# Expert sums held in four PSUM banks, one pool for the pre-activations, and a freed row buffer, in a one-core attention, retention and mixture-of-experts block

## The chip, the cores and the metric

The kernel runs on one core of one Trainium2 chip. The metric is the device time of one execution in microseconds. All numbers below come from three timed runs of the kernel before and from one profiled execution of it.

## The reference, cut to what matters

One transformer layer over 256 tokens of width 1024, in float32. The front part (attention over selected keys beside retention, one output projection, residual) is followed by a mixture of experts, and that is where nearly all the time goes:

```python
h2 = rms_norm(x, norm2_gain)
logits = h2 @ w_router + b_router             # 32 experts
top_val, top_idx = lax.top_k(logits, 4)       # each token goes to 4 of them
combine = one_hot(top_idx) weighted by softmax(top_val)
for e in range(32):
    z = h2 @ w1[e] + b1[e]                    # 1024 x 2048
    glu = minimum(z[..., 0::2], 7); lin = clip(z[..., 1::2], -7, 7)
    act = glu * sigmoid(1.702 * glu) * (lin + 1)
    out += combine[:, e] * (act @ w2[e] + b2[e])   # 1024 x 1024
x = rms_norm(x + out, final_gain)
```

The weights of an expert are 8 MB (w1) and 4 MB (w2), and all 32 experts are read once in a sweep: 402.7 MB.

## The kernel before, in words

**Stages.** The projections, the attention and the retention come first. TensorE then projects the output (L1272), the residual goes into `acc`, ScalarE copies it in another column order into `h2` (`copy_half`, L558), the router picks four experts for each token, and `place` (L875) gives each token a rank among the tokens of its expert. A sweep over the 32 experts follows; each has 64 slots, and a second sweep is run only if an expert has more tokens than that.

**One expert.** In `step` (L1469), for expert e, TensorE does, in an order written out by hand: the bias rows of z (`z_bias`, L1304), eight rows of w1 (`z_rows`, L1359; a "row" is 1 MB of weights, four matmuls), and between these rows the work of its neighbours: the gather of the tokens of expert e+1 (`gather`, L1344) and its transpose, the transpose of the activation of expert e-1 (`act_T`), the transposes of the gates, and after every second expert the scatter of the pair before (`scatter`, L1424). The step ends with `down` (L1384), the sixteen matmuls of w2 for expert e-1. VectorE reads z out of PSUM (`swiglu`, L961) and ScalarE applies the sigmoid and copies results out of PSUM.

**PSUM, before.** The z of even experts is in banks 0 and 1, that of odd ones in banks 2 and 3. The outputs of `down` and of the scatters share banks 4 and 5. After each scatter VectorE adds its 128x512 results to `acc` (`add_back`, L976), and TensorE waits for that. Only the last four experts are summed in PSUM, in banks 0 to 3: `final` opens these sums with zero matmuls (`open_sum`, L1442) and VectorE puts `acc` into them (`base_sum`, L1006).

**The weights' queue.** SyncE issues all weight loads in one order, each behind a wait for the buffer that it overwrites (`w1_used` counts rows of w1 that TensorE is done with, `w2_used` quarters of w2). w1 has 16 rows of buffer (two experts), w2 has four. By the time the experts begin, expert 0 and 1 are there, with w2 of expert 0 and one row of expert 2, which lies where a row of expert 0 would be; that row of expert 0 has a place in `arena`. From then on the queue goes by what TensorE frees: rows 0 to 6 of expert 2 as `w1_used` reaches 1 to 7, expert 3 at 9, 10, 12, 14 and 16, w2 of expert 1, the two halves of expert 4 at 20 and 24, w2, the halves of expert 5 at 28 and 32, and so on.

**The end.** `last_w2` (L325) puts w2 of experts 30 and 31 into rows of w1. `final` (L1517) runs the last expert and the last three `down`s. Then both token tiles are normalised and stored in four quarters, all issued by SyncE.

Of the kernel before, what the change touches and what calls it, by code (L numbers as in the profile page):

```python
# [21 lines left out]
P = 128  # L22
# [30 lines left out]
def constants():  # L53
# [12 lines left out]
    before = (np.arange(P)[:, None] < np.arange(P)[None, :]).astype(np.float32)  # L66
# [6 lines left out]
            "c_rank": np.concatenate([before, ones], 1), "c_onehot": onehot}  # L73


def hybrid_block(nc, x, norm1_gain, w_in, rel_bias, idx_k_ln_gain, idx_k_ln_bias, ret_gn_gain, w_out,
# [3 lines left out]
    with ctx:  # L80
# [10 lines left out]
        h2 = sb("h2", [P, TT, D])  # L91
# [29 lines left out]
        h2flat = h2[:, :, :].rearrange("p a b -> p (a b)")  # L121
        hT = carve(h2flat, 0, [KD, S])
# [42 lines left out]
        before, ones = carve(arena, 3400, [P]), carve(arena, 3528, [P])  # L165
# [49 lines left out]
        h2_ready = sem("h2_ready"); x2_tr = sem("x2_tr"); x2T_act = sem("x2T_act"); x2T_dve = sem("x2T_dve"); wr_ready = sem("wr_ready"); route_mm = sem("route_mm")  # L215
        top_ready = sem("top_ready"); ex_done = sem("ex_done"); chosen_ready = sem("chosen_ready")
        rank_mm = sem("rank_mm"); count_mm = sem("count_mm"); sweeps_ready = sem("sweeps_ready")
# [12 lines left out]
        gT_tr = sem("gT_tr"); gT_sb = sem("gT_sb"); scattered = sem("scattered"); added = [sem(f"added{t}") for t in range(TT)]  # L230
        shifted = sem("shifted")
        y_dve = sem("y_dve"); part_sum = sem("part_sum"); based = sem("based"); fin_sq = sem("fin_sq"); fin_inv = sem("fin_inv"); fin_root = sem("fin_root"); res_ready = sem("res_ready")
        last_dma = sem("last_dma")

# [13 lines left out]
        def _(sp):  # L248
# [26 lines left out]
            sp.dma_start(w1r[:, 6, :], w1_v[0, 1, 1, :, 0:2048]).then_inc(w1_in[3], 16)  # L275
            sp.dma_start(w1r[:, 7, :], w1_v[2, 1, 1, :, 2048:4096]).then_inc(w1_in[3], 16)
# [19 lines left out]
            sp.dma_start(before, c_rank[:, 0:P]).then_inc(rank_in, 16)  # L296
# [41 lines left out]
            def rest_of_sweep(base):  # L338
# [23 lines left out]
                by_row(3, 1, range(2))  # L362
                next_w1(base, 3, 1, range(1, 4))
# [34 lines left out]
            sp.wait_ge(fin_root, 3)  # L398
            sp.dma_start(out_v[:, 1, 512:1024], res[:, 1, 512:1024]).then_inc(last_dma, 16)
# [50 lines left out]
        def _(act):  # L450
# [105 lines left out]
            def copy_half(t, c):  # L556

                nc.scalar.activation(h2[:, t, :].rearrange("p (j c q) -> p c j q", j=4, c=2)[:, c],  # L558
                                     acc[:, t, 512 * c:512 * c + 512].rearrange("p (q j) -> p j q", j=4), ACT.Copy).then_inc(h2_ready, 1)

# [4 lines left out]
            copy_half(0, 0)  # L565
            copy_half(0, 1)
# [4 lines left out]
            copy_half(1, 0)  # L571
            copy_half(1, 1)
# [7 lines left out]
            for i in range(2):  # L580
                nc.scalar.activation(hg[:, 256 * i:256 * i + 256], ps[:, 4, 256 * i:256 * i + 256], ACT.Copy).then_inc(first_copied, 1)
# [3 lines left out]
            def take_hg(base, e):  # L585

                act.wait_ge(gathered, base + e)
                nc.scalar.activation(hg, ps[:, 6, :], ACT.Copy).then_inc(hg_sb, 1)  # L588
# [11 lines left out]
            def take_y(base, e, par):  # L600
                act.wait_ge(w2_used, 4 * base + 4 * (e + 1))
                lo = 64 * par
                nc.scalar.activation(ysb[lo:lo + 64, 0, :], ps[lo:lo + 64, 4, :], ACT.Copy)  # L603
                hi = 64 - lo
                nc.scalar.activation(ysb[hi:hi + 64, 1, :], ps[hi:hi + 64, 5, :], ACT.Copy).then_inc(y_sb, 1)

            def take_y_half(base, e, par, bank=4):
# [5 lines left out]
            def take_gateT():  # L613
                act.wait_ge(first_made, 3)
                nc.scalar.activation(gateT[:, :], ps[:, 4, 0:P], ACT.Copy).then_inc(first_copied, 1)

            def take_gT(half_base, m, to=gT):
                act.wait_ge(gT_tr, half_base + m + 1)
                nc.scalar.activation(to, ps[:, 6, :].rearrange("p (a n) -> p a n", a=2), ACT.Copy).then_inc(gT_sb, 1)

            def step(base, hb, m, par, first=False, last=False):
# [4 lines left out]
                if not (first and par == 0):  # L626
                    take_act(base, e - 1)
                if par == 1:
# [4 lines left out]
            def final(base, hb):  # L633
# [5 lines left out]
                take_y_half(base, NE - 3, 1)  # L639
                take_act(base, NE - 1, actT_last)  # L640
                nc.scalar.activation(spare[:, 0:1], spare[:, 1:2], ACT.Sqrt)
                take_y_half(base, NE - 2, 0)
                take_y_half(base, NE - 1, 1, bank=6)

            def sweep(base, hb, start=False):
# [3 lines left out]
                if start:  # L649
                    take_gateT()  # L650
# [18 lines left out]
            act.wait_ge(part_sum, 4 * n)  # L669
# [3 lines left out]
            act.wait_ge(scattered, n * NE)  # L673
# [5 lines left out]
            nc.scalar.activation(res[:, 1, 512:1024], res[:, 1, 512:1024], ACT.Copy, scale=st[:, 7:8]).then_inc(fin_root, 1)  # L679

        @block.vector
        def _(dve):
# [228 lines left out]
            def count_sweeps():  # L911

                dve.wait_ge(count_mm, 1)
                link(v.tensor_reduce(st[0:1, 76:77], ps[0:1, 5, 0:NE], AX.X, ALU.max))
# [46 lines left out]
            def swiglu(base, e, zb, free=True, lin=lin):  # L961
# [14 lines left out]
            def add_back(hb, j, t):  # L976

                for c in range(2):
# [630 lines left out]
```

## Time and profile before

| | |
|---|---|
| time of three runs | 1081.39, 1081.69, 1081.77 us; median 1081.69 |
| the profiled execution's own time | 1080.58 us |
| its span, first to last instruction | 1078.8 us (1.78 us lie around it) |
| TensorE matmul busy | 1037.1 us, 96% of the span |
| VectorE, ScalarE, GpSimd busy | 302.9, 157.0, 22.2 us |
| moved by DMA | 429.79 MB, mean 398 GB/s |
| mean granted TensorE clock | 0.988 |

Busy time of TensorE is not TensorE at its peak, and the page shows matmul busy and DMA busy both near full for most of the span: the table alone doesn't say which of the two sets the time of a stage. Waits and the pace of the loop do.

### The profile page before, as it was taken

The numbers are of one execution on the slowest core, as the hardware profiler recorded it, in microseconds if no ns is written. First come the engines' busy times: TensorE is split into PE (matmuls) and PEld (weight loads), VectorE is DVE, ScalarE is ACT, GpSimd is POOL, SyncE is SP. The second block draws the span as 40 slices with busy tenths as digits, with TensorE's granted clock in tenths as the row PEclk, the third lists the DMA queues.
The fourth block names the chain that finished last, engine by engine and source line by source line (L and its number), as shares of the span: only waits on it lengthen the run. The fifth ranks groups of instructions, "written<-read, shape, count | busy, mean of one in ns | idle before, by whom it ended". The sixth has DMA issues, their size and how long they took to land.

```text
span 1078.8 us, 11542 instructions
## 1 busy us (share of the span) xinstructions
PE 1037.1 (96%) x4616; PEld 400.2 (37%) x4616; DVE 302.9 (28%) x704; ACT 157.0 (15%) x282; POOL 22.2 (2%) x29
## 2 busy tenths in 40 slices
PE   8999999999999999999999999898989899999997
PEld 7458454333333333333333333332333333333332
DVE  2555622422222222222221312221223222221231
ACT  1231333110111111101010111011101101011111
POOL 1212000000000000000000000000000000000000
PEclk9999999999999999999998999999999999999999
DMA  9886948999999999999999999999999999999995
GB/s 327 244 254 263 385 166 317 396 435 425 427 426 433 435 428 433 430 428 429 434 433 430 432 427 433 433 435 430 429 431 434 434 430 429 435 434 431 423 426 235
DMA packets 33066, 429.79 MB, mean 398 GB/s; under 512 B 4908, under 2 KB 6352, under 8 KB 16368
## 3 DMA queue, kind: packets, MB, share of 16 engines
q1 hardware_dynamic: 31120, 426.03, 93.7%
q10 hardware_dynamic: 1216, 1.70, 1.1%
q0 software_dynamic: 704, 1.71, 0.6%
q8 instruction: 17, 0.28, 0.1%
q14 instruction: 9, 0.07, 0.0%
HBM read 426.80 MB, written 2.62 MB: 398 GB/s over the span
## 4 chain that ended last, share of the span: by engine, by line
PE 67%; DMA 30%; DVE 1%; issue 1%; SPq 0%; ACT 0%; ACTq 0%; DVEq 0%
PE ps L1370 28%; DMA w1r<-w_mlp 23%; PE ps L1398 13%; DMA w2r<-w_mlp 6%; PE ps L1439 5%; PE ps L1348 3%; PE ps L1099 3%; PE ps L1111 3%; DMA w1r<-w_out 1%; PE ps L1166 1%; PE ps L1412 1%; PE ps L1272 1%; PE ps L1131 1%; PE ps L1241 1%; PE ps L1356 1%; PE ps L1378 1%
## 5 line engine op out<-in xcount | busy, mean ns | idle before, releaser
L1370 PE MATMUL ps<-w1r,arena 128*64 128x512 f32 x2040 | 483.5, 610 | 22.4 <-DMA w1r<-w_mlp 22.1
L1370 PEld LDWEIGHTS ps<-w1r,arena 128*64 128x64 f32 x2040 | 141.9, 139 | 283.7 <-issue 277.3
L1398 PE MATMUL ps<-w2r,arena 128*64 128x512 f32 x960 | 212.1, 593 | 7.6 <-DMA w2r<-w_mlp 7.6
L1398 PEld LDWEIGHTS ps<-w2r,arena 128*64 128x64 f32 x960 | 68.2, 137 | 147.3 <-issue 131.4
L982 DVE TENSOR_TENSOR acc<-ps,acc 128x512 f32<-128x512 f32 x56 | 36.1, 686 | 173.5 <-PE ps L1439 173.5
L974 DVE TENSOR_TENSOR arena<-arena 128x512 f32<-128x512 f32 x32 | 22.2, 692 | 163.5 <-ACT arena L594 163.4
L598 ACT ACTIVATE arena<-ps 128x512 f32<-128x512 f32 x31 | 18.5, 597 | 288.7 <-PE ps L1378 288.6
L936 DVE TENSOR_TENSOR arena<-ps,cols 128x512 f32<-128x512 f32 x31 | 21.4, 692 | 139.1 <-PE ps L1356 139.1
L1348 PE MATMUL ps<-h,arena 128*64 128x512 f32 x248 | 58.7, 592 | 0.0
L603 ACT ACTIVATE arena<-ps 64x512 f32<-64x512 f32 x29 | 17.2, 592 | 269.6 <-PE ps L1398 269.6
L1439 PE MATMUL ps<-arena 128*128 128x512 f32 x112 | 55.5, 618 | 0.0
L957 DVE TENSOR_SCALAR arena<-small,rank,gate 128x64 f32<-128x64 f32 x128 | 31.3, 309 | 58.1 <-PE ps L1466 58.1
L588 ACT ACTIVATE arena<-ps 128x512 f32<-128x512 f32 x31 | 18.5, 597 | 158.4 <-PE ps L1348 158.4
L968 DVE TENSOR_SCALAR arena<-ps 128x512 f32<-128x512 f32 x32 | 33.5, 1048 | 13.2 <-PE ps L1370 13.2
L927 DVE TENSOR_SCALAR sel_z<-small 96x64 bf16 (+1 forms) x30 | 5.7, 190 | 103.1 <-PE ps L1370 103.1
L969 DVE TENSOR_SCALAR arena<-ps 128x512 f32<-128x512 f32 x32 | 33.9, 1061 | 0.0
L1439 PEld LDWEIGHTS ps<-arena 128*128 128x128 f32 x112 | 19.0, 189 | 36.0 <-issue 36.0
L1348 PEld LDWEIGHTS ps<-h,arena 128*64 128x64 f32 x248 | 18.8, 137 | 34.9 <-issue 34.3
L1111 PE MATMUL ps<-h,w1r 128*128 128x256 f32 x128 | 28.1, 380 | 0.0
L1099 PE MATMUL ps<-w1r,h 128*128 128x512 f32 x64 | 27.8, 592 | 0.0
L1111 PEld LDWEIGHTS ps<-h,w1r 128*128 128x128 f32 x128 | 24.2, 190 | 3.3
L1378 PEld LDWEIGHTS ps<-small,arena 128*128 128x128 f32 x128 | 13.4, 140 | 26.0 <-issue 26.0
(259 smaller groups left out, 604.1 us busy)
## 6 DMA issues: line engine op xcount, KB each, us to landing
w1r<-w_mlp SPq DMA_DIRECT2D x54, 4096.0 KB, 30.9
w2r<-w_mlp SPq DMA_DIRECT2D x32, 2048.0 KB, 18.1
w2r<-w_mlp SPq DMA_DIRECT2D x14, 4096.0 KB, 20.5
w1r<-w_mlp SPq DMA_DIRECT2D x17, 2048.0 KB, 9.6
w1r<-w_in SPq DMA_DIRECT2D x6, 2048.0 KB, 19.0
w1r<-w_mlp SPq DMA_DIRECT2D x12, 1024.0 KB, 7.8
w1r<-w_out SPq DMA_DIRECT2D x2, 2048.0 KB, 13.8
w1r<-w_in SPq DMA_DIRECT2D x2, 1024.0 KB, 10.6
```

Source lines behind the costliest of these rows:

```text
L957: ins = v.tensor_scalar(gated[:, t, which, at:at + 64], slotn, rank[:, t, bass.ds(e, 1)], gate[:, t, bass.ds(e, 1)], ALU.is_equal, ALU.mult)
L968: v.tensor_scalar(g3, z[:, :, :, 0], 7.0, None, ALU.min).then_inc(glu_ready, 1)
L969: v.tensor_scalar(l3, z[:, :, :, 1], 7.0, -7.0, ALU.min, ALU.max).then_inc(z_read, 1)
L974: v.tensor_tensor(lin, lin, sig, ALU.mult).then_inc(act_ready, 1)
L982: ins = v.tensor_tensor(sl, ps[:, 4 + c, :], sl, ALU.add)
L1099: ins = mm(ps[:, bank + t, 0:n], hT[:, k, P * t:P * t + P], w[:, k, 0:n], start=(k == 0), stop=(k == KD - 1))
L1111: ins = mm(ps[:, bank + g // 2, S * (g % 2):S * (g % 2) + S], w[:, k, P * g:P * g + P], hT[:, k, :], start=(k == 0), stop=(k == KD - 1))
L1348: ins = mm(ps[64 * c:64 * c + 64, 6, :], onehotP[:, par, t, :], h2[:, t, :].rearrange("p (j c q) -> p c j q", j=4, c=2)[:, c], start=(t == ...
L1370: ins = mm(ps[64 * c:64 * c + 64, 2 * par + n, :], hgT[:, par, k % 4, 64 * (k // 4):64 * (k // 4) + 64], cols_z, start=False, stop=(k == 7))
L1378: ins = nc.tensor.transpose(ps[:, 7, P * j:P * j + P], lin[:, P * j:P * j + P], ident)
L1398: ins = mm(ps[at:at + 64, 4 + c, :], actT[:, k % 4, 64 * (k // 4):64 * (k // 4) + 64], w2r[:, k // 2, col:col + 512], start=(k == 0), stop ...
L1439: ins = mm(ps[:, 4 + c, :], gT[:, c, P * t:P * t + P], ysb[:, c, :], start=not with_bias, stop=True)
```

## The change

1. **z in one pair of banks.** z of every expert is in banks 4 and 5 (expert 1 alone in 2 and 3, `z_bank`). `z_bias` of an expert now waits until VectorE has read z of the expert before. `down` writes both halves into bank 6; gather, transposes and gate transposes share bank 7.
2. **Sums in banks 0 to 3 from the first scatter on.** `open_sum` and `base_sum` run once, inside expert 2's step. Every scatter adds to these banks; `add_back` and the waits on it are gone.
3. **`h2` is gone.** Gathers read `acc` directly, and ScalarE puts the columns in order when it copies the gathered tokens out of PSUM (`take_hg`, and the two first copies, now with a stride of four elements). The freed buffer, `hx`, holds a row of expert 0; expert 2's last pair of rows is loaded as a whole beforehand. At `w1_used` 7 `hx` takes row 7 of expert 3, and row 6 of expert 3 is issued at `w1_used` 15 in place of a pair at 16.
4. **Around the start.** Ranks count the tokens behind instead of ahead, which gives the count per expert with one small VectorE operation in `place` and spares two matmuls. The z bias of expert 1 moves ahead of the first expert, `gate_T` into expert 1's step behind row 6. `keep_busy` matmuls stand at a few places of the front part.
5. **The end.** A new order in `final`; the pair 28 is added at the end of expert 30's step; the last quarter of the output is issued by ScalarE.

```diff
+        def z_bank(base, e):
+            return 2 if isinstance(base, int) and isinstance(e, int) and e == 1 else 4
...
             sp.wait_ge(proj_done, 5)
-            sp.dma_start(w1r[:, 6, :], w1_v[0, 1, 1, :, 0:2048]).then_inc(w1_in[3], 16)
-            sp.dma_start(w1r[:, 7, :], w1_v[2, 1, 1, :, 2048:4096]).then_inc(w1_in[3], 16)
+            load_w1(2, 3, 3)
...
             sp.wait_ge(proj_done, 8)
             load_w1(0, 2, 2)
+            sp.dma_start(hx[:, :], w1_v[0, 1, 1, :, 0:2048]).then_inc(w1_in[3], 16)
...
                     sp.wait_ge(w1_used, 7)
-                    sp.dma_start(w1r[:, 6, :], w1_v[2, 1, 1, :, 0:2048]).then_inc(w1_in[3], 16)
+                    sp.dma_start(hx[:, :], w1_v[3, 1, 1, :, 2048:4096]).then_inc(w1_early, 16)
+                    by_row(3, 1, range(2))
+                    next_w1(base, 3, 1, range(1, 3))
+                    sp.wait_ge(w1_used, 15)
+                    sp.dma_start(w1r[:, 14, :], w1_v[3, 1, 1, :, 0:2048]).then_inc(w1_in[7], 16)
...
-            sp.wait_ge(fin_root, 3)
-            sp.dma_start(out_v[:, 1, 512:1024], res[:, 1, 512:1024]).then_inc(last_dma, 16)
...
-            copy_half(0, 0)
-            copy_half(0, 1)
...
             for i in range(2):
-                nc.scalar.activation(hg[:, 256 * i:256 * i + 256], ps[:, 4, 256 * i:256 * i + 256], ACT.Copy).then_inc(first_copied, 1)
+                nc.scalar.activation(hg[:, 256 * i:256 * i + 256].rearrange("p (j q) -> p j q", j=2),
+                                     ps[:, 0, :].rearrange("p (q j) -> p j q", j=4)[:, 2 * i:2 * i + 2], ACT.Copy).then_inc(first_copied, 1)
...
+            act.wait_ge(fin_root, 3)
+            act.dma_start(out[0].rearrange("(t p) d -> p t d", p=P)[:, 1, 512:1024], res[:, 1, 512:1024]).then_inc(last_dma, 16)
...
                 dve.wait_ge(mm_done, count)
+                if t == TT - 1:
+                    v.tensor_tensor(lw[0:1, 0, 0:NE], ps[0:1, 6, 64 + NE:64 + 2 * NE], chosen[0:1, t, :], ALU.add)
...
-            def add_back(hb, j, t):
...
+            def base_sum(t):
+
+                dve.wait_ge(opened, t + 1)
+                v.tensor_copy(ps[:, 2 * t:2 * t + 2, :].rearrange("p b n -> p (b n)"), acc[:, t, :]).then_inc(based, 1)
...
+            def keep_busy(n, bank):
+
+                for i in range(n):
+                    mm(ps[:, bank, :], bias3[:, 0:P], bias3[:, 0:512], start=True, stop=True)
...
             gather_first(1).then_inc(first_made, 1)
-            mm(ps[:, 5, 0:NE], ones, chosen[:, 0, :], start=True, stop=False)
-            mm(ps[:, 5, 0:NE], ones, chosen[:, 1, :], start=False, stop=True).then_inc(count_mm, 1)
+            z_bias(0, 1, 1, free=False)
...
+            keep_busy(1, 0)
...
                 if free:
-                    pe.wait_ge(z_read, base + e - 1)
+                    pe.wait_ge(z_read, base + e)
...
                 for c in range(2):
-                    ins = mm(ps[:, 4 + c, :], gT[:, c, P * t:P * t + P], ysb[:, c, :], start=not with_bias, stop=True)
-                ins.then_inc(scattered, 1)
+                    ins = mm(ps[:, 2 * t + c, :], gT[:, c, P * t:P * t + P], ysb[:, c, :], start=False, stop=False)
...
+                if isinstance(base, int) and isinstance(m, int) and (m, par) == (1, 0):
+                    pe.wait_ge(first_copied, 3)
+                    for t in range(TT):
+                        open_sum(t)
...
+                if par == 1 and first and isinstance(base, int):
+                    gate_T()
                 if par == 1:
                     gates_T(base, hb, m)
...
+                if last:
+                    pe.wait_ge(y_sb, base + e - 1)
+                    pe.wait_ge(gT_sb, hb + m)
+                    for t in range(TT):
+                        add_expert(t, 0, gT)
```

`final` on TensorE after the change, from its start (`add_expert` is two matmuls over 64 rows, `down_late` the `down` from rows of w1):

```python
z_bias(base, e, 1)
for k in range(5): z_rows(base, e, lap, k, 1, False)
act_T(base, e - 1)
for k in range(5, 7): z_rows(base, e, lap, k, 1, False)
gates_T(base, hb, NE // 2 - 1)
z_rows(base, e, lap, 7, 1, False)
down(base, wb, e - 2, 1)
act_T(base, e, lin_last)
down_late(0, 0, actT_30, range(4), {0: 0}, hb, 4)
for t in range(TT): add_expert(t, 1, gT)
down_late(0, 0, actT_30, range(4, 8), {4: 1}, hb, 4)
down_late(1, 4, actT_last, range(4), {0: 2}, hb, 5)
add_expert(0, 0, gT_last)
down_late(1, 4, actT_last, range(4, 8), {4: 3, 6: 4, 7: 5}, hb, 5)
add_expert(1, 0, gT_last)
add_expert(0, 1, gT_last, stop=True)
add_expert(1, 1, gT_last, stop=True)
```

## Rows read from the trace of the kernel before

**Rows 1.** The page, GB/s of the DMA engines in 40 slices of 27 us
```profile
GB/s 327 244 254 263 385 166 317 396 435 425 427 426 433 435 428 433 430 428 429 434 433 430 432 427 433 433 435 430 429 431 434 434 430 429 435 434 431 423 426 235
```

**Rows 2.** The chain that ended last: start, us, what; first rows of a step
```profile
347.16 3.44 PE ps L1370 x16
...
400.49 3.44 PE ps L1370 x16
...
685.25 3.65 PE ps L1370 x16
...
743.53 5.35 PE ps L1370 x16
```

**Rows 3.** Stretches: length, busy us of PE, PEld, DVE, ACT, POOL, granted clock, DMA share, GB/s
```profile
740.00:750.00 10.00, 7.72 (x31) 2.75 (x29) 0.69 (x1) 1.70 (x3) 0.00 (x0) 0.83 1.01 436
135.00:140.00 5.00, 5.00 (x16) 2.32 (x15) 0.00 (x0) 0.00 (x0) 0.00 (x0) 1.00 0.00 0
204.00:208.00 4.00, 4.00 (x21) 1.48 (x21) 1.64 (x8) 0.60 (x1) 0.00 (x0) 1.00 0.94 332
226.00:262.00 36.00, 36.00 (x162) 12.13 (x160) 8.16 (x16) 4.09 (x7) 0.00 (x0) 1.00 1.00 429
262.00:266.00 4.00, 4.00 (x20) 1.29 (x18) 3.28 (x6) 0.00 (x0) 0.00 (x0) 1.00 1.00 393
```

**Rows 4.** SyncE's queue, single issues in order of time: start, us
```profile
206.92 0.33 SPq L255 DMA_DIRECT2D w1r<-w_mlp  x1
210.35 0.33 SPq L258 DMA_DIRECT2D w2r<-w_mlp  x1
...
222.80 0.33 SPq L309 DMA_DIRECT2D w1r<-w_mlp  x1
...
262.35 0.33 SPq L309 DMA_DIRECT2D w1r<-w_mlp  x1
```

**Rows 5.** Groups by line and shape, ScalarE, 150 to 172 us: busy us, mean ns
```profile
L558 ACT ACTIVATE h<-acc 128x512 f32<-128x512 f32 x4 | 4.3, 1112 | 0.0
L547 ACT ACTIVATE arena<-acc 128x512 f32<-128x512 f32 x4 | 2.5, 628 | 7.8 <-DVE acc L850 7.8
...
L581 ACT ACTIVATE arena<-ps 128x256 f32<-128x256 f32 x2 | 0.7, 380 | 0.3 <-PE ps L1299 0.3
```

**Rows 6.** Instructions in order of time, all engines, start of expert 1
```profile
188.14 0.42 PE L1421 MATMUL ps<-small,gate 128*32 128x128 f32 x8
188.24 0.69 DVE L936 TENSOR_TENSOR arena<-ps,cols 128x512 f32<-128x512 f32 x1 [15.57 <-PE ps L1356]
188.49 0.62 PE L1310 MATMUL ps<-bias,sel_z 96*64 96x512 bf16 x4
...
188.99 3.65 PE L1370 MATMUL ps<-w1r,arena 128*64 128x512 f32 x16
...
189.74 0.17 DVE L914 TENSOR_REDUCE st<-ps 1x1 f32<-1x32 f32 x1
```

**Rows 7.** Instructions in order of time, all engines, the last 55 us
```profile
1024.41 0.60 PE L1310 MATMUL ps<-bias,sel_z 96*64 96x512 bf16 x4
...
1025.53 1.08 DVE L969 TENSOR_SCALAR arena<-ps 128x512 f32<-128x512 f32 x1
...
1031.81 0.60 PE L1445 MATMUL ps<-bias 96*128 96x512 bf16 x2
...
1046.01 3.65 PE L1398 MATMUL ps<-w2r,arena 128*64 128x512 f32 x16 [0.21 <-DMA w2r<-w_mlp]
...
1067.70 2.33 PE L1458 MATMUL ps<-arena 64*128 64x512 f32 x8
...
1069.96 1.98 PE L1451 MATMUL ps<-arena 128*128 128x512 f32 x4
...
1074.44 0.72 ACT L679 ACTIVATE w1r<-w1r,st 128x512 f32<-128x512 f32 x1 [0.23 <-DVE st L1060]
1075.85 0.45 SPq L399 DMA_DIRECT2D out<-w1r  x1
```

More of the change, by code:

```diff
@@ L988, in step @@
                 if not (first and par == 0):
-                    swiglu(base, e - 1, 2 * (1 - par), free=not (first and par == 1))
-                if par == 1 and not first:
-                    add_back(hb, m - 1, 0)
+                    swiglu(base, e - 1, z_bank(base, e - 1), free=not (first and par == 1))
+                if residual:
+                    base_sum(0)
                 take_hgT(base, e + 1, 1 - par)
-                if par == 1 and not first:
-                    add_back(hb, m - 1, 1)
+                if residual:
+                    base_sum(1)
                 if par == 1:
@@ L1041, in sweep @@
                 step(base, hb, 0, 1, first=True)
-                with dve.Fori(1, NE // 2 - 1) as m:
+                step(base, hb, 1, 0, residual=start)
+                step(base, hb, 1, 1)
+                with dve.Fori(2, NE // 2 - 1) as m:
                     step(base, hb, m, 0)
@@ L1092, in _ @@
                     if t == 0 and g == 0:
+                        for i in range(2):
+                            mm(ps[:, 0, 0:S], zeros[:, 0:P], zeros, start=True, stop=True)
                         pe.wait_ge(gain_in, 48)
@@ L1323, in _ @@
             pe.wait_ge(chosen_ready, 1)
-            mm(ps[:, 6, 64:64 + NE], before, chosen[:, 0, :], start=True, stop=True).then_inc(rank_mm, 1)
+            mm(ps[:, 6, 64:64 + NE], behind, chosen[:, 0, :], start=True, stop=True).then_inc(rank_mm, 1)
             x2_T(1, 1)
@@ L1329, in _ @@
             pe.wait_ge(chosen_ready, 2)
[L1330 removed]
+            mm(ps[:, 6, 64 + NE:64 + 2 * NE], behind, chosen[:, 1, :], start=False, stop=True).then_inc(rank_mm, 1)
             pe.wait_ge(bias_part, 3)
@@ L1357, in gather_T, with z_rows @@
                 ins.then_inc(hg_tr, 1)
-            def z_rows(base, lap, k, par, halves, early=None, row=None):
+            def z_rows(base, e, lap, k, par, halves, early=None, row=None):
                 if halves and k % 4 == 0:
@@ L1479, in step @@
                 else:
-                    z_bias(base, e, par, free=not first)
+                    if not (first and isinstance(base, int)):
+                        z_bias(base, e, par, free=not first or par == 1)
                     pe.wait_ge(hgT_sb, base + e + 1)
-                z_rows(base, lap, 0, par, halves, early=4 * rb + 4 if isinstance(m, int) and (m, par) == (1, 0) else None)
-                z_rows(base, lap, 1, par, halves)
+                z_rows(base, e, lap, 0, par, halves, early=4 * rb + 5 if isinstance(m, int) and (m, par) == (1, 0) else None)
+                z_rows(base, e, lap, 1, par, halves)
                 if par == 0 and not first:
@@ L1519, in final @@
                 e, lap = NE - 1, rb * 3 + 3
+                z_bias(base, e, 1)
                 pe.wait_ge(hgT_sb, base + e + 1)
-                z_bias(base, e, 1)
-                for k in range(4):
-                    z_rows(base, lap, k, 1, False)
-                pe.wait_ge(z_read, base + e)
-                open_sum(0)
-                for k in range(4, 6):
-                    z_rows(base, lap, k, 1, False)
+                for k in range(5):
+                    z_rows(base, e, lap, k, 1, False)
@@ L1528, in final @@
                 act_T(base, e - 1)
+                for k in range(5, 7):
+                    z_rows(base, e, lap, k, 1, False)
                 gates_T(base, hb, NE // 2 - 1)
-                for k in range(6, 8):
-                    z_rows(base, lap, k, 1, False)
-                pe.wait_ge(based, 2 * rb + 1)
-                pe.wait_ge(y_sb, base + e - 2)
-                add_expert(0, 0, gT)
-                down(base, wb, e - 2, 1, ks=range(4))
+                z_rows(base, e, lap, 7, 1, False)
```

195 lines of the change are left out of this document (76 added, 119 removed).

## The prediction, on record before the result

> **What bounds the kernel now.** I read the page's DMA line first, then the chain, then SyncE's queue against stretches of the DMA rate. From 216 us on the weights flow at 423 to 436 GB/s [rows 1], while the chain shows two paces: a pair of experts takes 53.33 us at 347 us and 58.28 us at 685 us [rows 2]. A pair is 25.17 MB, so 58.28 us is 432 GB/s: late in the run the weights' flow sets the pace. At 53.33 us TensorE sets it and eats up a lead of loaded weights. So the end is set by when the flow was last interrupted, plus the bytes left, plus what TensorE does after the last awaited weights. Where was that? Between 135 and 140 us nothing flows, and there are holes up to 208 us; from 226 to 262 us it is full at 429, then 262 to 266 us shows 393, a last hole of about 0.35 us [rows 3]. It is where the second half of expert 5 is issued, at 262.35 us [rows 4], when TensorE is done with the last row of expert 3. After that the flow has more work than it can do. The balance agrees: from the issue at 206.92 to that at 262.35 us, 22 loads' worth of 1 MB are queued (2, 4, 8, 4 and 4), 23.07 MB or 53.4 us. The 2 MB before them start in the hole of 204 to 208 us, say 205.3, and last 4.9 us, so the 22 are through at 263.6 us, just as the next load can begin. Before 262 us the rate of TensorE therefore counts one for one, after it hardly at all until 1046 us, where w2 of expert 29 lands and TensorE waits 0.21 us for it [rows 7]. From there TensorE and the last stores run without waiting for weights.
>
> **The freed row.** One MB more is loaded ahead of the experts, in the empty stretch of 135 to 140 us, so it costs nothing there (2.43 us of 5). Worth: 1.049 MB / 432 GB/s = 2.43 us, if the flow were full afterwards. It isn't. With 21 MB queued instead of 22 the flow would be through at 261.1 us and wait for the issue at 262.35 us all the more; the new hole opens earlier too, at about 222 us, ahead of the issue now at 222.80 [rows 4]. The last awaited event is the same row of expert 3, so I put the row at 0, with 2.43 us as its upper bound.
>
> **The start of the experts.** Each of these delays TensorE, thus `w1_used`. (a) The first gathered tokens are now copied with a stride of four. The nearest rows are `copy_half`, which reads SBUF with this stride, 1112 ns for 512 columns, against 628 ns for the plain read of `acc`; the two copies here are 380 ns for 256 each [rows 5]. Half of 484 ns is +0.24 on the first copy; from PSUM it could be 0 or twice that. The second copy is late by twice as much, and behind its transposes stands a `keep_busy` matmul ahead of row 0: together they hold row 0 another 0.05 to 0.3. (b) The extra VectorE operation in `place` is bounded by 0 and the 0.17 us of a 1x32 operation on PSUM [rows 6]: +0.1. Sum of the start: +0.4, between 0.1 and 1.0. Dropping `copy_half` gains nothing: ScalarE was free again before the gather ended (it then waited 0.3 us) [rows 5]. The two count matmuls lay beside the copy, and so does the z bias of expert 1 now.
>
> **Expert 1 to 3.** Moving `gate_T` and the z bias out of the start of expert 1 gains nothing: both lie from 188.14 to 188.99 us, beside VectorE's copy of hgT from 188.24 to 188.93 that row 0 waits for [rows 6]. But `gate_T` comes back behind row 6 with 0.35 us (188.14 to 188.49), and the four zero matmuls of `open_sum` are new within expert 2: two are 0.60 us busy [rows 7], four at pace some 1.0 (bounds 0.8 and 1.2). Sum: +1.35 at the issue of 262.35 us. The base copies on VectorE lie beside rows 3 to 6 of expert 2. With the start, that issue and all flow after it come 1.75 us later (0.9 to 2.4; subtract up to 0.35 for the hole that was there).
>
> **The loop.** The 56 adds of `add_back` leave VectorE, which was not the bound; TensorE never waited for them in the stretch up to 430 us. z in one pair of banks: the wait on z_read is covered by the sixteen matmuls of `down`, 6.9 us by the pace of 3.44 us for eight [rows 2], against 2.2 us that VectorE needs (1024.4 to 1026.6) [rows 7]. If that cover failed it would be 2.2 us an expert, as it is once, below. `down` into one bank: `z_rows` does that already at the same pace. The slower `take_hg` (about 1.1 us) has rows 2 and 3 to hide behind, 3.4 us. So 0, with perhaps 0.3 either way.
>
> **The end, before w2 of expert 29.** Without a `down` in expert 30's step, the z bias of expert 31 waits for z_read: the two adds put there take about 2.0, the wait ends at 1026.7 in place of 1024.41 [rows 7]: +2.3. Taken away before 1046.01: two `open_sum`s and one add, 0.5 + 0.6 + 1.1 = 2.2. TensorE had 0.2 us to spare, so it arrives about as the weights land. 0, up to +0.5.
>
> **The end, after it.** Before: from 1046.01 to the last sum at 1071.94, 25.9 us. In the new order, by the rows: the rest of `down` 3.45, `act_T` 0.6, four half `down`s at 3.5, five steps of adds. An add of two 64-row matmuls is half of 2.33, at most 1.1 [rows 7]; six of them remain, 6.6. Sum 3.45 + 0.6 + 14.0 + 6.6 = 24.6; half a wait for the last copies, which now lie behind an add, gives 24.65. I take -1.3 (-0.3 to -2.2). The last weights still land in time: they were some 1 us ahead of their matmuls.
>
> **The last store.** ScalarE was done with it at 1075.16 (1074.44 + 0.72), SyncE issued it at 1075.85 behind another [rows 7]. Issued by ScalarE itself: -0.5, at least -0.1, at most -0.7. By the Trainium skill (DMA: Bandwidth & Descriptors, Issuing engines are not separate DMA queues) another issuing engine saves only the sequencer's time of the issue. By that rule the gain is the 0.45 us of one issue, the sum the same within 0.05 us.
>
> The same page (Anatomy of one DMA) gives a fixed cost of about 2.0 us per DMA, most of it completion. That rule speaks against the new queue: a load issued into an empty flow pays it. No sum here uses it, because the last hole ends the same delay after its issue in both kernels; by the rule the new hole near 224 us would be about 2 us longer than the bytes say, with no effect on the end.
>
> **Sum.** +0.4 + 1.35 + 0 + 0 - 1.3 - 0.5 = -0.05 us against the profiled 1080.58, which lies 1.1 below the median of the runs. Less some 0.2 for the small hole that was there before, I predict 1081.4 for the median, with its own range 1079.8 to 1083.0. 0.2% is 2.2 us, about what a measurement of this kernel can tell from no change.
>
> **The rivals.** (1) *The freed row counts.* The flow after 262 us was already behind, the hole of 0.35 us is scatter of the rate, and 2.43 us come off less the start's and inserts' 1.75 at most. For it: 393 against 429 over 4 us is little. Against: the balance above, which closes within 0.3 us. If the flow was not starved, the end comes by -2.43 - 1.8 = -4.2 at the most (1077.5); if only half, 1079. Chance of a result under -2.2: 0.20. (2) *A low clock at the end.* After waits of 2.3 us for weights the granted clock fell in some cases: 0.83 at 740 to 750 us, and two rows took 5.35 us in place of 3.65 [rows 2, 3], the rate of 1.2 GHz for a while. If TensorE comes to w2 of expert 29 more than 2.3 us early (it was warm at expert 29, or the adds cost less), the waiting is free but the low clock behind it is not: +1.7 to +3.4, as nothing covers TensorE there, total +1.6 to +3.3 (1083.3 to 1085). Against: it comes 0.2 us early now. It decides from 2.3 us early on. Chance 0.07. (3) *The tail gains nothing*, because the last weights arrive later than the reordered rows want them or the copies of y are exposed: +1.3 (1083.0), chance 0.13, within 0.2%. The forecast itself: 0.60.
>
> So faster 0.20, same 0.73, slower 0.07. The range takes the freed row's bound at the bottom and the lower edge of the clock's case at the top: 1077.8 to 1083.4.
>
> **What the profile after would show.** Row 0 of expert 0 starting 0.4 us later; the issue after row 32 about 1.75 us later; a hole of 2 to 4 us in the flow near 224 us and one at 264 us; w2 of expert 29 landing 1.5 us later; 24.6 us from there to the last sum. I am wrong if that landing comes earlier than before, if the inserts cost much more than 1.35 us, or if VectorE's reading of z holds TensorE in every step.

## The result, and the profile after

The changed kernel takes 1083.88 us (median of 12 runs, 1082.81 to 1087.86), the kernel before 1081.63 (12 runs, 1080.27 to 1084.06). The ratio is 1.0027, with a 95% interval of 1.0019 to 1.0034: slower by 2.9 us (2.1 to 3.7). The medians alone differ by 2.25 us. I had forecast 1081.4 and a range up to 1083.4. The profiled execution took 1084.49 us with a span of 1082.7, against 1080.58 and 1078.8: the two profiles differ by 3.9 us, 1 us more than the runs do.

I followed the prediction's steps through the trace of after. First the start of expert 0 and the work put into experts 1 and 2 (instructions in order of time, TensorE; start, duration, lines 1362 `z_rows`, 1413 `gate_T`, 1433 `open_sum`):

```profile
172.15 2.37 PE L1362 MATMUL ps<-w1r,arena 128*64 128x512 f32 x10
...
204.56 0.42 PE L1413 MATMUL ps<-small,gate 128*32 128x128 f32 x8
...
221.54 1.04 PE L1433 MATMUL ps<-bias 96*128 96x512 bf16 x4
```

Row 0 was at 171.95 before, so the start costs 0.2 us in this pair of traces. That is within the scatter of single executions: over the traces of the experiments below as well, e6_dve_order's left out, it begins at 171.6 to 172.0 us in the three with the old front part and at 171.5 to 172.2 in the eight with the new one. Next the issues of SyncE that answer to [rows 4]:

```profile
210.91 3.76 SPq L260 DMA_DIRECT2D w2r<-w_mlp  x2
224.48 8.67 SPq L311 DMA_DIRECT2D w1r<-w_mlp  x2
236.26 3.76 SPq L260 DMA_DIRECT2D w2r<-w_mlp  x2
251.83 12.53 SPq L311 DMA_DIRECT2D w1r<-w_mlp  x2
```

The row of 251.83 holds two issues, the second about 12.2 us behind the first, as in the kernel before (250.15 for the pair, 262.35 for its second). So the last hole in the flow is at 264.0, 1.68 us later; 1.75 was forecast. Counted from row 0 to the first issue behind row 24 it is 52.33 us in place of 50.85: the work put into experts 1 and 2 costs 1.48 us, and the start the other 0.2. The stretches of the flow around it (columns as in [rows 3]; the last is GB/s):

```profile
222.00:223.00 1.00, 1.00 (x7) 0.29 (x7) 0.82 (x1) 0.00 (x0) 0.00 (x0) 1.00 0.62 262
223.00:224.00 1.00, 1.00 (x8) 0.27 (x4) 0.41 (x1) 0.00 (x0) 0.00 (x0) 1.00 0.31 131
224.00:225.00 1.00, 1.00 (x10) 0.46 (x6) 0.00 (x0) 0.00 (x0) 0.00 (x0) 1.00 0.04 16
...
262.00:268.00 6.00, 6.00 (x30) 2.06 (x30) 4.20 (x10) 0.60 (x1) 0.00 (x0) 1.00 0.90 355
```

The row of weights gained by the freed buffer does empty the queue before 224.48, as argued: at 224 us nearly nothing flows. The small hole behind 262 us is there too and has grown: 355 GB/s over 6 us, where the trace of before has 404. So far the forecast holds. That of the end does not (TensorE in order of time; 1390 is `down`, 1404 `down_late`, 1440 `add_expert`; this answers to [rows 7]):

```profile
1044.43 3.60 PE L1390 MATMUL ps<-w2r,arena 128*64 128x512 f32 x16
1048.25 3.65 PE L1390 MATMUL ps<-w2r,arena 128*64 128x512 f32 x16 [0.22 <-DMA w2r<-w_mlp]
1051.84 0.66 PE L1370 MATMUL ps<-small,arena 128*128 128x128 f32 x4
1053.22 3.65 PE L1404 MATMUL ps<-w1r,b2f 128*64 128x512 f32 x16 [0.72 <-DMA w1r<-w_mlp]
1056.80 1.99 PE L1440 MATMUL ps<-arena 64*128 64x512 f32 x8
1058.72 3.65 PE L1404 MATMUL ps<-w1r,b2f 128*64 128x512 f32 x16
1063.03 3.65 PE L1404 MATMUL ps<-w1r,arena 128*64 128x512 f32 x16 [0.65 <-DMA w1r<-w_mlp]
...
1071.25 2.94 PE L1440 MATMUL ps<-arena 64*128 64x512 f32 x12
```

w2 of expert 29 lands 2.24 us later (1048.25 against 1046.01). From there to the last sum (1071.25 + 2.94 = 1074.19) it is 25.94 us, as before (25.93), and not 24.65: TensorE now waits twice for weights of the last two experts, 0.72 and 0.65 us, 1.37 in all, which in this execution is the whole forecast gain of 1.3.

Behind the last sum (VectorE, ScalarE and its queue in order of time; in brackets the idle time before the instruction and what ended it):

```profile
1071.37 0.68 DVE L1000 COPY arena<-ps 64x512 f32<-64x512 f32 x1 [8.25 <-PE ps L1404]
...
1075.22 0.69 DVE L1054 TENSOR_TENSOR w1r<-ps,w1r 128x512 f32<-128x512 f32 x1 [3.16 <-issue]
...
1077.67 0.72 ACT L676 ACTIVATE w1r<-w1r,st 128x512 f32<-128x512 f32 x1 [0.23 <-DVE st L1045]
...
1078.42 0.40 ACTq L678 DMA_DIRECT2D out<-w1r  x1
```

VectorE starts on the result 1.03 us after the last sum, and what ended its idle time is "issue", no other engine. The chain of that stretch says where it was (start, us, what; DVEq is VectorE's sequencer):

```profile
1071.37 0.56 DVE arena L1000
...
1072.28 0.07 DVEq L1036
1072.35 2.80 issue
1075.15 0.02 DVEq L1053
```

Line 1036 is the branch past the further sweeps (`dve.If(n > 1)`). After it VectorE's sequencer runs nothing for 2.80 us. Before, the same branch was there, behind the same copy:

```profile
1067.81 0.68 DVE L1004 COPY arena<-ps 64x512 f32<-64x512 f32 x1 [6.48 <-PE ps L1412]
1071.98 0.69 DVE L1069 TENSOR_TENSOR w1r<-ps,w1r 128x512 f32<-128x512 f32 x1 [3.49 <-PE ps L1451]
```

There the copy ended 3.45 us ahead of the last sum (1068.49 to 1071.94), and a gap of some 3.16 us fits within it; the trace of before can't show it, as VectorE had nothing to do sooner. In the new order the copy ends only 2.14 us ahead (1072.05 to 1074.19), and 1.03 us stick out. From the last sum to ScalarE's last product it is 4.20 us, before 3.22.

The account of the two profiles: last sum +2.25, behind it +0.98, stores to the end of the span +0.67 (4.31 against 3.64), sum 3.90 against 3.9 measured. The experiments are to show which of these belong to the change.

### The profile page after: what moved, and what is told of

Read it like the earlier page. It is cut to its first block, busy times and chain, and to the rows that moved or that the text cites. A ratio compares the mean times of both kernels' runs of the same rounds, so it can differ in the third digit from the quotient of the medians.

```text
span 1082.7 us, 11460 instructions
## 1 busy us (share of the span) xinstructions
PE 1036.8 (96%) x4628; PEld 400.4 (37%) x4628; DVE 265.9 (25%) x649; ACT 153.1 (14%) x278; POOL 22.2 (2%) x29
## 4 chain that ended last, share of the span: by engine, by line
PE 64%; DMA 33%; DVE 1%; issue 1%; SPq 1%; ACT 0%; DVEq 0%
DMA w1r<-w_mlp 27%; PE ps L1362 26%; PE ps L1390 12%; PE ps L1428 5%; DMA w2r<-w_mlp 4%; PE ps L1341 3%; PE ps L1091 3%; PE ps L1103 3%; DMA w1r<-w_out 1%; PE ps L1158 1%; PE ps L1267 1%; PE ps L1123 1%; PE ps L1233 1%; PE ps L1348 1%; PE ps L1370 1%
## 5 line engine op out<-in xcount | busy, mean ns | idle before, releaser
L1362 PE MATMUL ps<-w1r,arena 128*64 128x512 f32 x2024 | 477.2, 607 | 23.5 <-DMA w1r<-w_mlp 22.6
L1390 PE MATMUL ps<-w2r,arena 128*64 128x512 f32 x960 | 212.1, 593 | 10.2 <-DMA w2r<-w_mlp 10.2
L1341 PE MATMUL ps<-acc,arena 128*64 128x512 f32 x248 | 58.7, 592 | 0.0
L1341 PEld LDWEIGHTS ps<-acc,arena 128*64 128x64 f32 x248 | 18.9, 137 | 34.4 <-issue 33.8
L1103 PE MATMUL ps<-hx,w1r 128*128 128x256 f32 x128 | 28.1, 380 | 0.0
L1091 PE MATMUL ps<-w1r,hx 128*128 128x512 f32 x64 | 27.8, 592 | 0.0
L1103 PEld LDWEIGHTS ps<-hx,w1r 128*128 128x128 f32 x128 | 24.2, 190 | 3.3
L971 DVE SCALAR_TENSOR_TENSOR arena<-arena 128x512 f32<-128x512 f32 x32 | 22.2, 692 | 1.1
```

What stands on the lines that cost most here:

```text
L971: v.scalar_tensor_tensor(lin, lin, 1.0, glu, ALU.add, ALU.mult).then_inc(prod_ready, 1)
L1091: ins = mm(ps[:, bank + t, 0:n], hT[:, k, P * t:P * t + P], w[:, k, 0:n], start=(k == 0), stop=(k == KD - 1))
L1103: ins = mm(ps[:, bank + g // 2, S * (g % 2):S * (g % 2) + S], w[:, k, P * g:P * g + P], hT[:, k, :], start=(k == 0), stop=(k == KD - 1))
L1341: ins = mm(ps[64 * c:64 * c + 64, 7, :], onehotP[:, par, t, :], acc[:, t, 512 * c:512 * c + 512], start=(t == 0), stop=(t == TT - 1))
L1362: ins = mm(ps[64 * c:64 * c + 64, z_bank(base, e) + n, :], hgT[:, par, k % 4, 64 * (k // 4):64 * (k // 4) + 64], cols_z, start=False, stop ...
L1390: ins = mm(ps[at:at + 64, 6, :], actT[:, k % 4, 64 * (k // 4):64 * (k // 4) + 64], w2r[:, k // 2, col:col + 512], start=(k == 0), stop=(k ...
```

## The experiments

The theory at this point: the end is set by TensorE's progress at 262 us, one to one; the freed row is worth nothing; the end's new order would give its gain, but two waits and the gap behind the branch take it. Rivals: late slack counts as well; the row counts and hid a bigger loss; the store by ScalarE or the flow itself is at fault.

Each ratio below is to the kernel before and has about 1 us of interval to each side. Two of them can be told apart from some 1.3 us on. So the 0.9 to 1.1 us by which e4, e6 and e7 come out under the changed kernel are not clear of noise one by one: that each edit takes away the wait or the gap that it aims at is read from its trace, and that this brings the time back is shown by e8, which has two of the edits and is clear of noise.

**e1_delay_early and e2_delay_late.** The kernel before, with sixteen idle bf16 matmuls (nothing of the result depends on them) in expert 2, or in expert 6. For e2 the loop over experts 4 to 7 is written out as well, so that one of them can be picked:

```diff
                 z_rows(base, lap, 2, par, halves)
+                if isinstance(base, int) and isinstance(m, int) and (m, par) == (1, 0):
+                    pe.wait_ge(z_read, e)
+                    idle_work(16, 2)
```

In e2 the pair in the condition is (3, 0).

> The kernel before with sixteen extra bf16 matmuls of 512 columns (3.4 us at 0.21 us each) on TensorE inside expert 2, ahead of the last row of expert 3. Their results are never used. Theory (the weights' flow last ran dry at the second half of expert 5, which waits for expert 3's last row): all 3.4 us come back at the end, the issue at 262.35 us moves by 3.4 us, w2 of expert 29 lands 3.0 to 3.4 us later, total +3.0 to +3.5 us. Rival (the flow was not dry there, the weights' bytes alone set the end): under 1 us.

> The kernel before with the same sixteen matmuls inside expert 6, behind the last time the flow ran dry. Theory: the lead of TensorE over the weights is eaten anyway, so 0 (within 0.5 us), w2 of expert 29 lands when it did. Rival (TensorE's work counts everywhere): +3.4 us, as in the early place.

Measured: e1 1085.91 us, ratio 1.0036 (1.0023 to 1.0050), +3.9 us; e2 1082.62, ratio 1.0005 (0.9996 to 1.0014), within the interval nothing. The idle matmuls of e1, the issue that waits until 24 rows of w1 are used (at 222.80 before [rows 4]), and w2 of expert 29:

```profile
220.66 3.63 PE L1445 MATMUL ps<-bias 96*128 96x512 bf16 x16
...
226.19 8.67 SPq L309 DMA_DIRECT2D w1r<-w_mlp  x2
...
1050.30 3.65 PE L1398 MATMUL ps<-w2r,arena 128*64 128x512 f32 x16 [0.40 <-DMA w2r<-w_mlp]
```

In e2 the last of these stands near its old place, 1046.01:

```profile
1046.57 3.65 PE L1398 MATMUL ps<-w2r,arena 128*64 128x512 f32 x16 [0.25 <-DMA w2r<-w_mlp]
```

In e1 the issue comes 3.39 us later and w2 of expert 29 4.29, more than the 3.0 to 3.4 expected; the time grows by 3.9 (2.5 to 5.4). The same matmuls in expert 6 move the time by 0.5 us (-0.4 to 1.5), which leaves no room for the rival's 3.4. Early work counts in full and late work doesn't, as the balance of the flow in the prediction has it. The landing scatters by itself: from the last issue of the early stretch (the second half of expert 5) to w2 of expert 29 it is 783.0 to 784.6 us in the seven traces in which TensorE waits for that w2.

**e3_no_row.** The changed kernel with the freed buffer used for expert 0's row only; the loads of experts 2 and 3 are in the order of before.

```diff
-                    sp.dma_start(hx[:, :], w1_v[3, 1, 1, :, 2048:4096]).then_inc(w1_early, 16)
+                    sp.dma_start(w1r[:, 6, :], w1_v[2, 1, 1, :, 0:2048]).then_inc(w1_in[3], 16)
...
-                sp.dma_start(w1r[:, 14, :], w1_v[3, 1, 1, :, 0:2048]).then_inc(w1_in[7], 16)
```

> The changed kernel without the use of the freed row: row 6 of expert 2 is loaded behind expert 0's row 6 again, row 7 of expert 3 with its pair behind the last row of expert 1. Theory (the freed row is worth nothing, as the flow runs dry at 224 and 264 us anyway): within 0.5 us of the changed kernel, so +2.2 us or so against before; the hole at 224 us shrinks from about 2.6 us to under 0.6 us. Rival (the row is worth its 2.43 us): 2.4 us slower than the changed kernel, +4.7 us against before.

Measured: 1084.41 us, ratio 1.0029 (1.0017 to 1.0041), 0.2 us from the changed kernel's with 1.5 to each side; the row's 2.43 us are ruled out. The issue behind row 24, and then the rate of the flow ahead of it (last column):

```profile
224.27 8.67 SPq L311 DMA_DIRECT2D w1r<-w_mlp  x2
```

```profile
223.00:224.00 1.00, 1.00 (x6) 0.14 (x2) 0.19 (x1) 0.00 (x0) 0.00 (x0) 1.00 0.92 393
224.00:225.00 1.00, 1.00 (x8) 0.62 (x8) 0.15 (x1) 0.00 (x0) 0.00 (x0) 1.00 0.88 377
```

Without the extra row the queue is not empty at 224 us (393 and 377 GB/s in place of 131 and 16), and the issue comes when TensorE says, with the row or without. Over 222 to 227 us the changed kernel's flow is 2.8 us short of a full one at 430 GB/s and e3's 0.7, against 2.6 and under 0.6 expected: the row is spent in that hole. It is worth 0 as far as can be measured.

**e4_few_inserts.** The changed kernel, with `gate_T` and `open_sum(0)` in the wait for VectorE's copy at the start of expert 1. `gate_T` writes bank 6 for it in place of bank 0 and is no longer behind row 6; `open_sum(1)` stays in expert 2.

```diff
                 step(base, hb, wb, rb, 0, 0, first=True)
+                if start:
+                    gate_T()
+                    open_sum(0)
                 step(base, hb, wb, rb, 0, 1, first=True)
```

> The changed kernel with gate_T and the opening of the sums of the first token tile moved into the wait at the start of expert 1 (bank 6 in place of bank 0 for the gates). 0.35 + 0.43 us leave the busy part of experts 1 to 3. Theory: the issue at 264.03 us comes 0.7 to 0.8 us earlier, and so does the end; total +1.4 us against before. Rival (the later flow is not tied to that issue): no change to the end.

Measured: 1082.90 us, ratio 1.0017 (1.0008 to 1.0026), 1.1 us less than the changed kernel by the ratios, 1.3 to each side. The two fill the wait, and the issue comes 1.0 us earlier than 224.48; 0.75 of it is the edit's, as row 0 began 0.24 us earlier in this execution:

```profile
188.09 0.43 PE L1413 MATMUL ps<-small,gate 128*32 128x128 f32 x8
188.45 0.60 PE L1433 MATMUL ps<-bias 96*128 96x512 bf16 x2
188.99 3.22 PE L1362 MATMUL ps<-w1r,arena 128*64 128x512 f32 x14
...
223.49 8.67 SPq L311 DMA_DIRECT2D w1r<-w_mlp  x2
```

So the inserts cost what the rows said at the issue. That they count to the end agrees with the time and is shown by e1; this run alone doesn't show it.

**e5_sp_store.** The changed kernel with the last quarter issued by SyncE again (`act.dma_start` of line 678 becomes `sp.dma_start`, behind the same semaphore).

> The changed kernel with the last quarter stored by SyncE again, as before. In the profiles the time from the end of the last quarter's scaling to the end of the span was 3.64 us before and 4.3 us with ScalarE's store. Theory A (the two issues meet and SyncE's third one is slowed from 0.35 to 0.93 us): 0.3 to 0.7 us shorter than the changed kernel. Theory B, that of the prediction (a parallel issue saves the 0.45 us): 0.5 us longer.

Measured: 1083.54 us, ratio 1.0030 (1.0018 to 1.0043): 0.3 us above the changed kernel, with 1.5 to each side, so the time tells neither theory's half us from nothing. The traces say more. From the end of the last quarter's scaling to the end of the span it takes 3.6 to 4.8 us in the five traces in which SyncE issues the last quarter and 3.9 to 4.9 in the seven in which ScalarE does, 4.4 on the mean in both. No gain and no loss by the issuing engine shows there, and the 3.64 against 4.31 of the first two profiles are scatter. For the flow of the four quarters see e10_all_sp.

**e6_dve_order.** The changed kernel with VectorE's copy of the last expert's output behind its branch, so that the branch is passed while TensorE still works. (A sweep past the first takes its copy inside the branch.)

```diff
                 take_y_half(base, NE - 2, 0, 4)
-                take_y_half(base, NE - 1, 1, 5)
...
+            dve.wait_ge(w2_used, n * (4 * NE))
+            v.tensor_copy(ysb[0:64, 1, :], ps[0:64, 5, :]).then_inc(y_dve, 1)
```

> The changed kernel with VectorE's copy of the last expert's output moved behind the branch on the number of sweeps. In the profile of the changed kernel VectorE's instruction behind that branch starts 3.16 us after the copy, 1.0 us after the last sum is there. Theory (the gap is the branch and what it fetches, formerly hidden behind 3.5 us of matmuls): the multiplication with the gain starts within 0.1 us of the last sum, 1.0 us less. Rival (VectorE waits for something else, such as the load of the gain): the gap stays.

Measured: 1083.17 us, ratio 1.0019 (1.0009 to 1.0028), 0.9 us less by the ratios, 1.3 to each side. The gap is gone: VectorE now starts 0.10 us after the last sum, which ends at 1073.99 + 2.94 = 1076.93, and what ended its wait is TensorE:

```profile
1077.03 0.69 DVE L1057 TENSOR_TENSOR w1r<-ps,w1r 128x512 f32<-128x512 f32 x1 [2.24 <-PE ps L1443]
```

**e7_tail.** The changed kernel with the sums of expert 29 ahead of expert 30's first late rows, and a semaphore each for the two rows of expert 31's first half, so that each weight is wanted a little later.

```diff
...
-                down_late(0, 0, actT_30, range(4), {0: 0}, hb, 4)
                 pe.wait_ge(y_sb, base + e - 1)
                 pe.wait_ge(y_dve, 3 * rb + 1)
                 for t in range(TT):
                     add_expert(t, 1, gT)
+                down_late(0, 0, actT_30, range(4), {0: 0}, hb, 4)
...
-                down_late(1, 4, actT_last, range(4), {0: 2}, hb, 5)
+                down_late(1, 4, actT_last, range(4), {0: 2, 2: 6}, hb, 5)
```

> The changed kernel with two edits at the end: the adds of expert 29 go ahead of the first half of expert 30's last matmuls, and the first half of w2 of expert 31 is loaded as two rows with a wait each. Theory (the new order's gain of 1.3 us was lost in two waits for weights of 0.72 and 0.65 us): both waits go, from w2 of expert 29 to the last sum it takes 24.5 us in place of 25.9, total 1.3 us less than the changed kernel. Rival (the adds cost more than I think, and the waits only hid it): under 0.3 us.

Measured: 1082.59 us, ratio 1.0017 (1.0007 to 1.0026), 1.1 us less by the ratios, 1.3 to each side. Both waits for weights are gone:

```profile
1044.92 7.04 PE L1394 MATMUL ps<-w2r,arena 128*64 128x512 f32 x32
...
1052.84 1.99 PE L1444 MATMUL ps<-arena 64*128 64x512 f32 x8 [0.30 <-DVE arena L1004]
1054.76 7.09 PE L1408 MATMUL ps<-w1r,b2f 128*64 128x512 f32 x32
1061.68 3.60 PE L1408 MATMUL ps<-w1r,arena 128*64 128x512 f32 x16
...
1069.85 2.93 PE L1444 MATMUL ps<-arena 64*128 64x512 f32 x12
```

Half of the `down` of 1044.92 is 3.52 us, so its second half begins at about 1048.44, and the last sum ends some 24.34 us later (1072.78). That is the forecast length of the new order or a little less (24.65, and 25.93 before).

The two waits are not the same in every execution of the changed kernel's order. Five traces have that order. After and e5 show both (0.72 and 0.65 us, 0.74 and 0.64). In e3, e4 and e6 TensorE comes to w2 of expert 29 after it has landed and waits for the last expert's alone, as in e3:

```profile
1062.67 3.65 PE L1400 MATMUL ps<-w1r,arena 128*64 128x512 f32 x16 [0.58 <-DMA w1r<-w_mlp]
```

From the last early issue to the last sum it is 810.2 us on the mean of the three traces with the old end, 809.7 of these five and 809.0 of the four with e7's edit, each trace within 0.8 us of its group's mean. So the new order alone gives some 0.5 us of the 1.3, and the edit gives the rest.

**e8_tail_dve, e9_all, e10_all_sp.** The edits together: e7 and e6; with e4; with e5.

> The changed kernel with both edits of the end together: the sums of expert 29 stand ahead of expert 30's late rows and expert 31's third and fourth rows of w_mlp2 have a semaphore each (e7_tail, -1.1 us against the changed kernel), and VectorE's copy of the last expert's output stands behind its branch (e6_dve_order, -0.9 us). Theory: the two losses are apart (two waits of TensorE for weights; a gap on VectorE after TensorE is done), so they add: -2.0 to -2.1 us, 1081.8 at the changed kernel's 1083.9, ratio to the kernel before 1.0008. Rival: both only move work against the same last transfer, so that one hides in the other: -1.1 us, ratio 1.0017.

> The same with the transposes of the gates and the opening of one pair of banks moved into a wait that TensorE has anyway at the start of expert 1 (e4_few_inserts, -0.9 us against the changed kernel). Theory: every early us counts one to one, so the three edits add: -3.0 us, 1080.9, ratio to the kernel before 0.9999 (0.999 to 1.0008), that is, no difference. Rival: once TensorE no longer waits for weights at the end, the transfers are what is late and the early 0.85 us gives nothing more: as e8_tail_dve. A second rival: the reordered end is faster than the one before (the gain of 1.3 us that was forecast) and comes on top: ratio 0.9988.

> e9_all with the last quarter stored by SyncE as in the kernel before. Theory: as e9_all within 0.2 us (e5_sp_store: no difference in the changed kernel, 1.003 against 1.0027). Rival: with the gap on VectorE gone, all four quarters become ready closer together and the fourth issue queues behind the third on SyncE: 0.4 to 0.9 us slower than e9_all.

| | us | ratio to before, 95% |
|---|---|---|
| e8_tail_dve | 1081.81 | 1.0004 (0.9995 to 1.0013) |
| e9_all | 1081.83 | 1.0003 (0.9994 to 1.0012) |
| e10_all_sp | 1081.79 | 1.0003 (0.9994 to 1.0013) |

e8 comes out at the sum of e6 and e7 or a little better (-2.5 us against the changed kernel, 1.3 to each side; -2.0 foreseen). The rival's -1.1 lies just outside that. Its trace has neither a wait for weights in the tail nor the gap, so the losses are apart. e9 should have been 0.9 us below e8 and is at the same time, though its trace has the early us: w2 of expert 29 at 1047.65, where e8 has the second half of that `down` at 1045.10 + 3.52 = 1048.62, and the last sum ends at 1072.13 against 1072.96. The spans are 1080.0 and 1080.9. With intervals of 1 us to each side, the times can neither show nor deny the 0.9. None of the three beats the kernel before; e9 gives back the loss and stands level with it.

e10 stores like the kernel before and is as fast as e9, within the 1.4 us to each side that the two ratios leave. The rate of the flow over the last 8 us, 40 slices of 0.2 us each, of e10 and then of e9:

```profile
GB/s 0 0 0 0 82 0 0 0 0 0 0 0 0 369 369 358 400 379 389 328 113 256 379 338 369 369 358 348 62 10 10 31 20 31 20 20 0 0 0 0
```

```profile
GB/s 0 82 0 0 0 0 0 0 0 0 0 0 0 236 389 389 359 400 410 348 82 195 430 358 389 348 358 359 133 10 10 31 20 31 20 20 0 0 0 0
```

The four quarters, 1.05 MB, flow almost without a break for 3 us, and then 10 to 31 GB/s trickle for another 1.4 us. A faster issue could at most close the low slice or two between the halves.

## Why the prediction was wrong, by its steps

*The flow as the bound, up to 262 us, and the freed row at 0:* right. The shift of the last issue was 1.68 against 1.75 (trace), early time counts and late time doesn't (e1, e2), the row moves the hole at 224 us and nothing that can be measured beyond it (e3). The fixed cost of 2.0 us that the prediction took from the Trainium skill stands there for DMAs issued by GpSimd, and SyncE issues these. The hole with the row is 2.1 us longer than without (2.8 against 0.7), less than the row's own 2.43, so no further 2 us show in it.

*The start, +0.4:* 0.2 in the trace, within the scatter. The copy out of PSUM with a stride of four takes what the plain one did: ScalarE is busy 0.66 us for the two halves in both traces. The nearest row, a strided read of SBUF at 1112 ns [rows 5], was the wrong neighbour. The same holds for `take_hg`, put at about 1.1 us: its 31 copies take 597 ns each, as before. *The inserts, +1.35:* 1.48, and e4 takes back 0.75 of it at the issue.

*The loop, 0:* right as far as the trace tells. Between 200 and 1050 us TensorE waits in the trace of after for weights alone (22.6 us for w1, 10.2 for w2), and never for VectorE's reading of z.

*The end, before w2 of expert 29, 0 to +0.5:* TensorE comes to it 0.22 us before it lands, as before (0.21); in e3, e4 and e6 it comes after the landing. No run takes this step by itself.

*The end, after it, -1.3, "The last weights still land in time":* this failed, and it is the rival that I gave 0.13. It gave 0 in the pair of profiles and some 0.5 us over all traces. The step counted TensorE's work from w2 of expert 29 on, and took the weights' lead from the old order, some 1 us for all of them. The trace of before has 2.8 us for the first half of expert 30's w2 (issued at 1011.12, 39.6 us to its landing, matmuls at 1053.57), but for expert 31's only 0.1 (1020.45, 40.1, and 1060.68): that one had no lead to spend. And the new order wants expert 30's w2 an add and a pair earlier: 4.25 us after w2 of expert 29 (1053.22 less 0.72 less 1048.25) where the old one came to it after 7.56 us [rows 7: 1046.01; the matmuls began at 1053.57]. It lands after 4.97. Expert 31's is wanted after 14.13 us and lands after 14.78. Every us saved after w2 of expert 29 is taken from that lead; two waits of 0.72 and 0.65 us came of it, and in every one of the five traces at least one of 0.57 us or more. e7's trace shows that it was the order and not the sum of the work: with both waits gone the end is some 24.34 us long. The kernel's 1.1 us less agree with it, and e8 makes them clear together with e6. The gain was real and stood behind a transfer.

*A term that was in no step, +1.0:* VectorE's pause behind its branch. The prediction asked what the copies of y hold up on TensorE, and not what VectorE has left to do after the last one. The trace of before has the 3.49 us of idle time with the last sum at its end, which reads as slack. By the 3.16 to 3.28 us that the gap takes in the five traces that show it, only 0.2 to 0.3 us of it was slack: a pause of the engine's own must have lain under the wait. e6 takes it off the end, for 0.9 us by the ratios and 0.93 in the traces (1.03 us from the last sum to VectorE's start, and 0.10). The Trainium skill (Runtime: NRT & Kernel Launch, Instruction fetch mechanics) says that a taken branch out of the loaded code stalls the engine until the code has been fetched. The trace agrees in so far as within the 2.80 us three packets with 0.03 MB of instructions are moved, two of them at 1073.0 to 1073.6. The trace doesn't name the engine they are for, but e6 helps: its branch is passed behind a copy that ends at 1065.91, and there one packet of 0.01 MB comes at 1066 to 1068 and one at 1070 to 1072, where the changed kernel has none, while behind the last copy (ended at 1074.78) only one such packet and one of 0.02 MB are left. So instruction traffic goes with VectorE's branch. That it is what fills the 2.80 us is argued; the pause behind the branch is shown.

*The last store, -0.5:* no gain in the traces (4.4 us on the mean with either engine), and none that the times can show (e5, and e10 against e9). The priced thing, 0.45 us of one issue, does not show at the end. With the end's gain gone, the pause on top and no gain at the store, the forecast becomes 1081.4 + 1.3 + 1.0 + 0.5 = 1084.2, outside the range; 1083.88 was measured. (The prediction's own times for its rivals, 1083.0 and 1083.3 to 1085, are counted from the 1081.7 of before and not from its forecast, and the upper bound of the early delay adds up to 2.55 us, not 2.4. Neither changes what follows.)

The sum by the two profiles: start 0.2, inserts 1.5, end's order 0, pause 1.0, store 0, together +2.7 us, inside the 2.1 to 3.7 of the ratio. The other 1.2 us between the profiles are scatter of single executions, as far as the runs tell. w2 of expert 29 comes 783.66 us after the last issue before and 784.22 after; with e5's trace, the same code there as the changed kernel's, it is 783.05 (1046.42 less 263.37). And the 3.64 us of stores in the trace of before are 4.26 in e2, which stores by the same code (1075.74 to 1080.0).

What stays open: whether the 0.9 us of e4 are there in e9, and how much of the 2.9 us each loss makes in measured time, as single edits of 1 us are at the edge of what these runs can tell.

## What to carry to other kernels

When an order is shortened behind an awaited transfer, check each later transfer for its lead: a saving behind the last wait is a demand that the next load land that much earlier. An idle engine whose wait ended with another engine's work may have a pause of its own under it; compare its idle time with what its sequencer did in the meantime (a branch, a register load) before calling it slack. And where one stretch alone counts, as the one up to 262 us here, put inserted work into waits of that stretch, not between its rows.

## What the runs showed of the hardware that I had not expected

VectorE's branch past the further sweeps was followed by 2.80 us in which its sequencer ran nothing, and by 3.16 to 3.28 us of idle time of the engine in five traces. ScalarE read PSUM with a stride of four at the pace of a plain read: 0.66 us for two copies of 128x256 and 597 ns for one of 128x512, the same in both kernels. SyncE's three issues of the last quarters took 337, 348 and 934 ns in the trace of after, for the same bytes each.

The profiled execution of e6 took 1086.35 us, its median is 1083.17. Its front part tells where the 3 us are (seventh number of a row, ahead of DMA share and GB/s: granted clock):

```profile
164.00:166.00 2.00, 1.80 (x16) 1.59 (x15) 1.37 (x4) 1.21 (x3) 0.00 (x0) 1.00 0.52 115
166.00:168.00 2.00, 2.00 (x17) 1.88 (x18) 0.89 (x4) 1.94 (x5) 0.00 (x0) 0.94 0.92 385
168.00:170.00 2.00, 2.00 (x6) 0.39 (x2) 0.75 (x6) 0.84 (x5) 0.00 (x0) 0.50 0.95 410
170.00:172.00 2.00, 2.00 (x10) 0.70 (x11) 1.33 (x7) 0.00 (x0) 0.00 (x0) 0.50 0.94 397
172.00:174.00 2.00, 2.00 (x10) 0.52 (x6) 0.00 (x0) 0.98 (x3) 0.00 (x0) 0.50 0.63 266
174.00:176.00 2.00, 1.97 (x11) 0.97 (x12) 1.20 (x4) 1.16 (x2) 0.00 (x0) 0.85 0.00 0
```

For some 6.8 us the clock was at 1.2 GHz in place of 2.4, after TensorE had been busy as in the other profiles (7.80 us of the 8 from 160 to 168 here, 7.74 to 7.80 in the other eleven, where the clock stays at 1.00). Its issue behind row 24 comes at 227.37, 2.9 us later than in the changed kernel, and the last sum ends 2.7 us later (1076.93 against 1074.19), which agrees with e1. Why the clock fell there in this execution and not in the others is open.
